# The forgetting heads' first loads of the prompt stage: issued by ACT in its own queue in place of SP's

## What is computed

```python
def attend_block(...):
    ...
    k_pos = jnp.arange(kf.shape[1], dtype=jnp.int32)
    decay = jnp.transpose(cq, (0, 2, 1))[..., None] - jnp.transpose(ck, (0, 2, 1))[:, :, None, :]
    lf = jnp.einsum('bqhd,bkhd->bhqk', q_f, kf).astype(jnp.float32) * scale + decay
    pf = masked_softmax(lf, k_pos[None, :] <= t_pos[:, None])
    o_f = jnp.einsum('bhqk,bkhd->bqhd', pf.astype(vf.dtype), vf).reshape(B, Q, FOX_HEADS * HEAD_DIM)
```

## Time and profile before

| What | Value |
|---|---|
| median of three runs | 1927.19 us (1925.48 to 1930.2) |
| the profiled execution | 1931.76 us |
| its span, first to last instruction | 1930.1 us |
| mean granted share of PE's clock | 0.967 |
| PE busy | 1808.7 us (94%) |
| DVE, ACT, POOL busy | 910.1, 576.5, 241.9 us |
| moved by DMA | 184.22 MB, mean 95 GB/s |

### The profile page before, as it was taken

The page is one execution under the profiler, slowest core; times in us unless marked ns, Lnnn a source line. Parts: engine busy times, 40 slices in busy tenths (PEclk is TensorE's granted clock), DMA queues, the critical chain, the costliest instruction groups (busy, mean ns, idle before and its releaser), DMA issues. The chain is left out here.

```text
span 1930.1 us, 34627 instructions
## 1 busy us (share of the span) xinstructions
PE 1808.7 (94%) x13317; PEld 1604.3 (83%) x13317; DVE 910.1 (47%) x1828; ACT 576.5 (30%) x1197; POOL 241.9 (13%) x547
## 2 busy tenths in 40 slices
PE   7889999899785999999998999999999999999998
PEld 6889999676463666667676889999999999999998
DVE  4423332125343776767775543333333332665655
ACT  4101010223232656565565640000000000344343
POOL 3000015400510322232221000000000000000000
PEclk9989999999996989999998999999999999999998
DMA  4434946745999012030201221111111110311112
GB/s 133 167 90 131 243 148 109 226 140 170 305 319 230 18 42 59 13 88 2 88 2 66 88 82 55 43 43 50 48 43 43 48 50 27 134 44 41 44 43 101
DMA packets 157263, 184.22 MB, mean 95 GB/s; under 512 B 23689, under 2 KB 120376, under 8 KB 157074
## 3 DMA queue, kind: packets, MB, share of 16 engines
q1 hardware_dynamic: 132658, 143.37, 24.5%
q0 software_dynamic: 11072, 30.78, 5.8%
q10 hardware_dynamic: 13408, 8.42, 2.0%
HBM read 152.30 MB, written 34.38 MB: 97 GB/s over the span
## 5 line engine op out<-in xcount | busy, mean ns | idle before, releaser
L183 PE MATMUL psum<-hf_hi,gu_hi 128*128 128x352 f32 x1056 | 341.1, 323 | 0.7 <-DVE gu_lo L2683 0.7
L184 PE MATMUL psum<-hf_lo,gu_hi 128*128 128x352 f32 x1056 | 338.8, 321 | 0.0
L185 PE MATMUL psum<-hf_hi,gu_lo 128*128 128x352 f32 x1056 | 338.6, 321 | 0.0
L183 PEld LDWEIGHTS psum<-hf_hi,gu_hi 128*128 128x128 f32 x1056 | 198.3, 188 | 1.0 <-DVE gu_lo L2683 0.9
L184 PEld LDWEIGHTS psum<-hf_lo,gu_hi 128*128 128x128 f32 x1056 | 198.6, 188 | 0.0
L185 PEld LDWEIGHTS psum<-hf_hi,gu_lo 128*128 128x128 f32 x1056 | 198.1, 188 | 0.0
L183 PE MATMUL psum<-x_hi,w_hi 128*128 128x352 f32 x528 | 173.0, 328 | 7.8 <-DVE w_lo L631 3.4
L183 PE MATMUL psum<-h_parts,down_hi 128*128 128x352 f32 x528 | 171.6, 325 | 8.6 <-ACT ffn_out L2630 5.5
L2014 ACT ACTIVATE probs<-psum,neg_max 128x640 f32<-128x640 f32 (+7 forms) x192 | 138.0, 719 | 119.9 <-DVE neg_max L2151 116.2
L184 PE MATMUL psum<-x_lo,w_hi 128*128 128x352 f32 x528 | 172.5, 327 | 0.0
L185 PE MATMUL psum<-x_hi,w_lo 128*128 128x352 f32 x528 | 172.4, 326 | 0.0
(11 more groups left out here) (377 smaller groups left out, 3169.9 us busy)
## 6 DMA issues: line engine op xcount, KB each, us to landing
fox_ring<-in_cache_fox_kv SPq DMA_DIRECT2D x128, 256.0 KB, 5.5
zT<-z_stage SPq DMA_DIRECT2D x22, 528.0 KB, 2.9
w_ring<-in_w_in POOLq DMA_DIRECT2D x22, 512.0 KB, 5.3
gu_ring<-in_w_ffn_gate SPq DMA_DIRECT2D x22, 512.0 KB, 3.8
gu_ring<-in_w_ffn_up SPq DMA_DIRECT2D x22, 512.0 KB, 3.9
down_ring<-in_w_ffn_down SPq DMA_DIRECT2D x44, 256.0 KB, 2.7
nsa_page<-in_cache_nsa_kv POOLq DMA_DIRECT2D x64, 128.0 KB, 6.4
out<-nat SPq DMA_DIRECT2D x12, 512.0 KB
```

The costliest lines, as they stand in the source:

```text
L183: nc.tensor.matmul(dst, w_hi, x_hi, start=start, stop=False)
L184: nc.tensor.matmul(dst, w_hi, x_lo, start=False, stop=False)
L185: return nc.tensor.matmul(dst, w_lo, x_hi, start=False, stop=stop)
```

## The change

The waits and issues of the forgetting heads' first tiles leave SP's stream, where they stood last, and stand in ACT's stream, ahead of its wait for the last transposed output and of its store. Order, sizes, targets and semaphores of the 11 DMAs are unchanged.

```diff
@@ build_b, block.sync
                 load_shared(sp, env, nsa_kv_prompt)
-                PE.wait(sp, ("use_v", RN - 1, 3))
-                load_fox_keys(sp, env, 0, env["fox_loaded"][0])
-                load_fox_rest(sp, env, fox_kv_prompt, 0)
@@ build_b, block.scalar
                     for k in range(3):
                         turn_done(("pt_fox", r, k))
+                PE.wait(act, ("use_v", RN - 1, 3))
+                load_fox_keys(act, env, 0, env["fox_loaded"][0])
+                load_fox_rest(act, env, fox_kv_prompt, 0)
                 DVE.wait(act, ("ev", ("ot_fox", RN - 1)))
                 with nc.allow_non_contiguous_dma(reason="four tokens of four sequences per head"):
                     store_fox(act, RN - 1, env["fox_out_last"])
```

## The result

The changed kernel is slower. Its median is 1940.12 us (five runs, 1937.05 to 1943.18), against 1925.93 us of the kernel before (five runs beside it, 1925.37 to 1930.2). The ratio of the runs is 1.0067, with a 95% interval of 1.0049 to 1.0084: 12.9 us, from 9.4 to 16.2 (0.0067, 0.0049 and 0.0084 of 1925.93). The forecast for the median was 1935.7 us and its range ended at 1941. In all ratios one run is left out: one of e7's twelve took 2549.04 us at a granted clock of 0.647.

The account below looks back on a forecast made before the run. It took PE to stand on the barrier and the 14 loads, the latter bound by the DMA engines; later landing +8.5, earlier barrier 0 and later work 0 gave 1935.7 us against the median 1927.19, range 1927 to 1941.

Parts of the forecast that it names:

- step one: At the stage boundary, PE stands on the barrier and the 14 loads, two waits ending within a microsecond or two.
- Rival 3: At PE's start: the barrier was the only real wait, so PE starts 8.3 us earlier, 1919 to 1921 us; chance 0.05.
- The earlier barrier is worth nothing: At the stage boundary: the barrier falls to between 590.7 and 597 us, counted as 0 because the other wait ends later.
- rival 4: At ACT's store: a full queue holds ACT and the barrier comes after 612 us, 1941 to 1945 us; chance 0.02.
- Issues on ACT: On ACT, from about 579 us: the 11 issues take about 6.5 us, until 586, and cost nothing directly.
- The loads' landing: At PE's first scores: two queues share busy DMA engines, so the 14 loads land at 606.5 us, 8.5 us later.
- equal shares of bytes: Case for the 14 loads' landing: both queues move equal bytes, landing at 607.3 us, PE starting 9.3 us later.
- turns of one DMA: Case for the 14 loads' landing: queues alternate whole DMAs, five of ACT's standing between SP's, giving 604 us.
- the 14 loads come last: Worst case for the landing: all 6.4 MB move first, landing at 611.8 us, 13.8 us later.
- Forgetting tiles in time: At the first forgetting scores: tiles wanted at 621.2 us land by 611.8 us even at worst, so nothing is added.
- The store and pair 1's loads later, covered: Behind ACT's loads: store and pair 1's loads come later, until some 635 us, with 70 us of cover before use.
- No gain or loss by the clock: After PE's start: its clock returns as long after the new start as the old, 3 us either way as uncertainty.

Follow-up runs that it names:

- e7: Changed kernel with q_fox and k_fox back on SP behind the 14 loads, ACT keeping decay rows and v_fox: 1933.54 us, ratio 1.0015 to the kernel before.
- e1: Kernel before, with SP issuing the 11 forgetting loads behind the barrier instead of ahead of it: 1928.48 us, ratio 0.999 to the kernel before.
- e4: Kernel before, with SP issuing keys, forgetting keys and decay rows ahead of the barrier, three value tiles behind it, separate semaphores: 1924.93 us, ratio 0.9971.
- e10: Changed kernel with v_slc and v_win on their own semaphore, waited for where values are first weighed: 1933.15 us, ratio 1.0001 to the kernel before.
- c_after: The changed kernel measured once more, without any edit: 1937.89 us, ratio 1.0042 to the kernel before.
- e2: Changed kernel with SP's values (v_slc, v_win) issued ahead of its keys: 1939.65 us, ratio 1.0046 to the kernel before.
- e3: Changed kernel with ACT's store issued ahead of its 11 loads: 1939.22 us, ratio 1.0052 to the kernel before.
- c_before: The kernel before, profiled once more without any edit: 1928.39 us in the profiled execution.
- e6: Changed kernel with the first pair's forgetting queries and keys asked for in 512 B pieces, which were joined again: 1939.95 us, ratio 1.0055 to the kernel before.
- e5: e4 with DVE preparing POOL's compressed-bias table earlier and POOL expanding it behind the barrier: 1922.62 us, ratio 0.9967 to the kernel before.
- e9: e5 with SP alone loading the two partition halves of each tile one after the other: 1922.45 us, ratio 0.995 to the kernel before.
- e8: e5 with SP loading the lower 64 partitions of keys and forgetting keys, ACT the upper: 1925.1 us, ratio 0.9969 to the kernel before.

## Why the prediction was right

**Two waits that end together: right.** PE now waits for v_win and the barrier is past earlier, as step one had it. e1 shows directly that 6.3 us behind the barrier the 14 loads are still missing. Rival 3, by which the barrier was the only real wait, is out by that row.

**The earlier barrier is worth nothing: right**, though not because SP's release set it. ACT's store, held 12.12 us, made ACT the last, to 595.57 us. I had priced this hold as hidden if it ends before the loads land; it ended 9.5 us before. And the lower bound that I gave the barrier, POOL's last work at 590.7 us, was too early: e1 and e4 show the barrier 4.9 us behind that work, which makes it 595.6 us. The gain that rival 3 reckoned with was thus 3.4 us at most (598.98 - 595.6), not 8.3. (A gain of 3.4 us lies inside e1's interval, so e1's time alone would not have ruled it out; its wait for v_win does.) e10 shows what it costs without that cover: there it is the wait that remains. That is rival 4's mechanism, with a hold of 14.87 us where that rival needed 25. The prediction had said that the store's issue moves little; it was held for 12.12 us.

**Issues on ACT: right.** 6.7 us for 6.5 forecast, from 576.75 us on, 2 us earlier than forecast in an execution whose stage ran 3.6 us ahead.

**The loads' landing: the mechanism right, the term mis-sized.** The forecast put PE's idleness at 12.73 + 8.5 = 21.2 us; it was 22.45, and 21.75 in c_after. That term, "later landing +8.5", measured 9.7 and 9.1 us. It was taken between equal shares of bytes (9.3) and turns of one DMA, as a guess on how two queues share. The runs put another order in its place: turns packet for packet, which the prediction had kept as its bound "the 14 loads come last", 13.8 us. It didn't cost 13.8, for two reasons. The first is the rate. Shifted by the 3.6 us that the stage ran ahead, the bound puts PE's start at 608.2 us (611.8 - 3.6); it started 3.1 us sooner, and 2.7 of these follow from the rate: from 577.4 to 604.4 us 6.60 MB moved, at 244 GB/s, where 222 would have needed 29.7 us in place of 27.0. The second is the base: I counted from 598 us, and PE had started at 598.98. 13.8 less 3.1 less 1.0 is the 9.7 that was measured. So the number came out near by luck: the order was worse than the middle value that I took, by 5.3 us, and rate and base were better, by 4.1.

The second queue's first packets also came later than I had allowed for: none of q10's between 578 and 583 us, and 22 between 583 and 584 us, though ACT issued at 576.75, so 6 us later, where I had allowed 2. In this order it changes nothing, because the bytes of both queues have to move before the last of the 14, whichever queue begins.

The Trainium skill, "DMA: Bandwidth & Descriptors", section "Queues, rings and completion order", says that a DMA engine takes turns between its queues packet by packet. The trace agrees, with 2096 packets of one queue against 2058 of the other; a packet of the trace is one piece here, since the values' packets hold 0.5 KB. In e2 and e3 the counts were not equal (532 against 136, 542 against 236), with SP held at its issues or few of its pieces left. I had weighed that rule and yet placed my number with equal bytes; followed to its end, with the sizes of pieces on both sides, it gives the order that the run showed.

**Forgetting tiles in time: right.** They had landed at 604.57 us, were wanted at 618.84, and PE's wait there is for ACT's exponent, 2.08 us as before (2.07).

**The store and pair 1's loads later, covered: right.** mixT was issued at 605.24 us, 6.4 us later than before, and pair 1 started with no wait.

**No gain or loss by the clock: right as far as two pairs of profiles can show.** From the first scores to the end of the span it is 1330.3 us against 1331.1, and in the second pair 1326.9 against 1330.9 (1931.4 - 604.46, 1926.7 - 595.84), where c_after's mean granted clock was 0.971 and c_before's 0.968. The first pair differs by 0.8 us, the second by 4.0, in the changed kernel's favour and inside the scatter of single runs. The first pair agrees although the windows' granted clock fell to 0.63 and 0.50 from 0.72 and 0.59.

**The sum against the median.** 1935.7 forecast, 1940.12 measured. In the difference to the run beside it the loss is 12.9 us in the first set and 8.1 in the second; the profiles show 9.7 and 9.1. What the first set shows beyond some 10 us I can't assign to a step; the second set makes scatter likelier than a missing term.

Still open: why the last of the values' pieces moved so slowly in e2 and e3, and whether smaller pieces in ACT's queue would have spared the values (e6 did not get them). That v_fox, in 512 B pieces, takes fewer bytes per turn fits e7, but e7 also has fewer bytes in all.

## What to carry to other kernels

Before moving loads to a second queue because its engine is free, ask whether the DMA engines are already busy, and compare the sizes of pieces: with turns taken packet for packet, a queue with 4 KB pieces took six times the bytes of one with 512 B pieces here (0.77 against 0.12 MB), whoever was more urgent. If they are busy, put the loads in order of need in one queue, and let each consumer wait for its own tiles by their own semaphore; here that, with no second queue, made the kernel 0.3% faster (e4; 0.3 and 0.5% in e5 and e9, where POOL's tables moved as well). When a wait is removed, look for the one that ends just behind it; here there were three within some 5 us (the barrier by POOL's end or a full queue, the values, the keys).

## What the runs showed of the hardware that I had not expected

- Between ACT's first issue (576.75 us) and the first packets of its queue (in the microsecond from 583 us) lay 6 us, while SP's queue kept the DMA engines busy. The kernel before has it too: its store was issued at 586.81 us and q10's first packets started after 592 us. In e2, e3, e7, e8 and e10 it was between 4 and 6.5 us.
- An issue can hold its engine for as long as the queue is full: 12.12 and 14.87 us for the two issues of ACT's store (11.45 and 14.20 for the first of the two), 9.64, 12.77 and 16.25 us for v_win of SP's. It delays not only what is queued behind it but the whole block's barrier: in e10 the hold ended at 600.99 us and PE started at 601.86.
- The barrier came 4.9 us after the end of POOL's last shown work (586.64 to 591.57 us in e1, 588.11 to 593.03 in e4), when no other engine was shown at work and no issue was held. In e5, where POOL had nothing left to do, it came 0.7 us after the last issue, ACT's store (588.87 to 589.54 us), and so it did in e8 and e9 (585.65 to 586.33 us, 590.12 to 590.79). So the 4.9 us go with POOL; of what they consist the profile doesn't show.
- Loads to 64 partitions at a time moved 212 to 222 GB/s from one queue, and 296 GB/s when two queues loaded opposite halves. The changed kernel's two queues moved 301 GB/s for 4 us (584 to 588 us) without such an order, and no run compares two queues on the same half, so the gain may belong to the second queue and not to the halves.
- Between 592 and 600 us in e3 SP's queue had 236 packets against 542 of ACT's: the one for one of the other kernels is not a fixed share of a queue.
